# Head 0's preparation in another order over eight banks, with two score tiles begun before the maximum row

## What the reference computes

```python
q = (rmsnorm(c_q, q_latent_g[l]) @ w_uq[l]).reshape(B, T, MLA_HEADS, QK_DIM)
kv = (rmsnorm(c_kv, kv_latent_g[l]) @ w_ukv[l]).reshape(B, T, MLA_HEADS, QK_NOPE + V_DIM)
...
q = rmsnorm(q, q_norm_g[l]); k = rmsnorm(k, k_norm_g[l])      # then rope on the last 32 columns
s = jnp.einsum('bqhd,bkhd->bhqk', qblk, k).astype(jnp.float32) * scale
p = jax.nn.softmax(s, axis=-1).astype(v.dtype)
return jnp.einsum('bhqk,bkhd->bqhd', p, v)
```

## Time and profile before

| | us |
|---|---|
| median of three runs | 1301.13 |
| lowest, highest | 1300.33, 1301.87 |
| the profiled execution | 1303.02 |
| its span | 1301.2 |
| PE busy in it | 1271.2 |

### The profile page before, as it was taken

One profiled execution on the slowest core, in us unless ns is written; L12 is line 12 of the kernel. 1 busy time (PEld: TensorE's weight loads), 2 busy tenths in 40 slices (PEclk: granted clock), 3 DMA queues, 4 the chain that ended last, 5 costly groups with the idle time before them and its releaser, 6 DMA issues.

```text
span 1301.2 us, 18506 instructions
## 1 busy us (share of the span) xinstructions
PE 1271.2 (98%) x6158; PEld 1018.6 (78%) x6158; DVE 996.9 (77%) x1505; ACT 769.3 (59%) x1156; POOL 146.6 (11%) x175
## 2 busy tenths in 40 slices
PE   7999999899999999999999999999999999999998
PEld 7999997666666666687678888888888888888886
DVE  6677569678887876577779887887878887887855
ACT  7487648567765866534445565656474565656460
POOL 3000037400000001322200000000010000000010
PEclk9999999999999999999999999999999999999999
DMA  6111200000000014200144846576574847576667
GB/s 220 34 53 41 74 1 1 1 1 10 9 9 10 9 58 155 69 30 1 49 148 94 187 100 166 118 169 134 151 169 93 189 97 169 113 170 133 157 143 245
DMA packets 40938, 123.01 MB, mean 95 GB/s; under 512 B 7378, under 2 KB 8082, under 8 KB 34484
## 3 DMA queue, kind: packets, MB, share of 16 engines
q0 software_dynamic: 7200, 52.43, 21.4%
q1 hardware_dynamic: 33684, 69.86, 15.7%
HBM read 62.34 MB, written 59.80 MB: 94 GB/s over the span
## 4 chain that ended last, share of the span: by engine, by line
PE 85%; DVE 6%; ACT 5%; issue 2%; DMA 1%; POOL 0%; SPq 0%; DVEq 0%; ACTq 0%
PE banks L2911 30%; PE banks L2983 14%; PE banks L100 7%; PE banks L102 7%; PE banks L101 7%; PE banks L1935 2%; PE banks L2040 2%; PE banks L2041 2%; PE banks L2042 2%; PE banks L2060 2%; PE banks L2063 2%; PE banks L2061 2%; ACT e_f L1558 1%; PE banks L1895 1%; ACT e_h L1565 1%
## 5 line engine op out<-in xcount | busy, mean ns | idle before, releaser
L2911 PE MATMUL banks<-x_hi,slot_h 128*128 128x512 f32 x616 | 242.8, 394 | 2.5 <-DVE slot_l L2599 1.3
L2911 PE MATMUL banks<-x_lo,slot_h 128*128 128x512 f32 x616 | 243.4, 395 | 0.0
L2911 PE MATMUL banks<-x_hi,slot_l 128*128 128x512 f32 x616 | 242.9, 394 | 0.0
L2384 ACT ACTIVATE slot_h<-up_raw 128x512 fp32r<-128x512 f32 x127 | 79.8, 629 | 174.4 <-PE banks L2911 172.3
L2911 PEld LDWEIGHTS banks<-x_hi,slot_h 128*128 128x128 f32 x616 | 115.6, 188 | 30.9 <-DVE slot_l L2599 2.1
L2911 PEld LDWEIGHTS banks<-x_lo,slot_h 128*128 128x128 f32 x616 | 115.7, 188 | 27.1
L2911 PEld LDWEIGHTS banks<-x_hi,slot_l 128*128 128x128 f32 x616 | 115.7, 188 | 26.9
L2462 ACT ACTIVATE staged<-banks 128x1024 f32<-128x1024 f32 x100 | 101.4, 1026 | 41.0 <-PE banks L2983 41.0
L2983 PE MATMUL banks<-dn_h,a_h 128*128 128x512 f32 x280 | 110.4, 394 | 0.0
L2983 PE MATMUL banks<-dn_h,a_l 128*128 128x512 f32 x280 | 109.5, 391 | 0.0
L2983 PE MATMUL banks<-dn_l,a_h 128*128 128x512 f32 x280 | 109.5, 391 | 0.0
(11 more groups left out here) (346 smaller groups left out, 2861.5 us busy)
## 6 DMA issues: line engine op xcount, KB each, us to landing
down_sums<-staged POOLq DMA_DIRECT2D x50, 1024.0 KB, 8.0
up_raw<-in_w_up SPq DMA_DIRECT2D x88, 256.0 KB, 3.3
dn_raw<-in_w_down SPq DMA_DIRECT2D x22, 512.0 KB, 6.6
win_raw<-in_w_in SPq DMA_DIRECT2D x11, 512.0 KB, 3.3
x_tm<-in_x_tm SPq DMA_DIRECT2D x8, 512.0 KB, 6.0
wo_raw<-in_w_out SPq DMA_DIRECT2D x16, 256.0 KB, 4.1
h<-in_x_tm SPq DMA_DIRECT2D x8, 512.0 KB, 5.7
down_sums<-h SPq DMA_DIRECT2D x3, 1024.0 KB, 6.6
```

The lines of the kernel that those rows point to most:

```text
L2384: nc.scalar.activation(s_h[slot], x, ACT.Copy).then_inc(sem["up_hi"], 1)
L2911: ins = nc.tensor.matmul(o, s[slot][:, k], xs[w], start=fresh and k == 0 and n == 0, stop=k == 3 and n == 2, skip_group_check=not fresh)
```

## The change

- The list ahead of head 0 is in another order: `tq0`, `tk0`, `a0`, `a1`, then `tq1`, `tk1`, `a2` to `a7`, `tm`, `a8` to `a15`, `am`, `r`. `x0` to `x2` of head 0 leave it; they are done in slots 1 and 2 of head 0, as for the heads behind.
- `side_banks` names the bank of every job: all eight ahead of head 0, 6 and 7 in turn behind. `before` is the last job ahead of it in the same bank.
- The waits on the projection's semaphores are given by job (`HEAD_0`).
- The identity products now stand before the job's own product: 4 at `tk0`, 4 at `a1`, 2 at each of `a2` to `a15`, 2 at `r`.
- `scores_ahead` makes the three products of all four halves of the score tiles of slots 0 and 1, without the 97th row, behind `r`. `scores` adds to each of them a product of the 97th rows alone once the row has come.

```diff
--- before.py
+++ after.py
@@ -1078,8 +1078,8 @@
                7: ("a14", "a15", "am", "r"), 8: ("", "", "", "")}
     LAST_AHEAD = dict(PREPARE)
     LAST_AHEAD.update({4: ("a5", "x0", "a6", "a7"), 5: ("a8", "x1", "a9", "a10"), 6: ("a11", "x2", "a12", "a13")})
-    FIRST = dict(PREPARE)
-    FIRST.update({8: ("x0", "x1", "x2", "")})
+    FIRST = {0: ("tq0", "tk0", "a0", "a1"), 1: ("tq1", "tk1", "a2", "a3"), 2: ("a4", "a5", "a6", "a7"),
+             3: ("tm", "a8", "a9", "a10"), 4: ("a11", "a12", "a13", "a14"), 5: ("a15", "am", "r", "")}
     OWN = {1: ("", "", "x0", "x1"), 2: ("", "x2", "", "")}
     META_QUERIES = {5: ("xt", "", "", ""), 8: ("", "", "", "xo")}
     LRU_SUMS = {1: ("ys", "", "", "")}
@@ -1091,7 +1091,7 @@
         places = [None] * 4
         ahead = FIRST if h < 0 else LAST_AHEAD if h == END - 1 else PREPARE
         for plan, head in [(ahead, h + 1), (META_QUERIES, h), (LRU_SUMS, h), (OWN, h)]:
-            if plan is OWN and not 1 <= h < END:
+            if plan is OWN and not 0 <= h < END:
                 continue
             if 0 <= head < HEADS and not (plan is META_QUERIES and h != END) and not (plan is LRU_SUMS and h != END - 2):
                 for i, kind in enumerate(plan.get(s, NONE)):
@@ -1104,8 +1104,10 @@
     jobs = [j for h, s in steps for j in side_jobs(h, s) if j]
     number = {j: n for n, j in enumerate(jobs)}
     first = len([j for s in range(SLOTS) for j in side_jobs(-1, s) if j])
+    side_banks = [2, 3, 6, 7, 0, 1, 4, 5] + [(6, 7, 4, 5, 2, 3, 0, 1)[n % 8] for n in range(first - 9)] + [4] +\
+                 [6 + n % 2 for n in range(len(jobs) - first)]
     BY_ACT = {"r", "x0", "x1", "x2"}
-    LOWS = [("tq0", 0), ("tq1", 0), ("tk0", 0), ("tk1", 0)]
+    LOWS = [("tq0", 0), ("tk0", 0), ("tq1", 0), ("tk1", 0)]
     full = [place(f"qk_full{n}", WORDS - 8 - 512 * (n + 1), (512,), parts=QK) for n in range(len(LOWS))]
     assert M_Z <= WORDS - 8 - 512 * len(LOWS)
 
@@ -1117,19 +1119,12 @@
 
     def side_of(j):
 
+        return bank(side_banks[number[j]], 1)
+
+    def before(j):
+
         n = number[j]
-        if n >= first - 3 and n < first:
-            return bank(4 + (n - first + 3) % 2, 1)
-        return bank([6, 7, 2, 3, 0, 1][n % 6] if n < first else 6 + (n - first) % 2, 1)
-
-    def before(j):
-
-        n = number[j]
-        if n < first - 3:
-            return jobs[n - 6:n - 5] if n >= 6 else []
-        if n < first:
-            return jobs[n - 2:n - 1] if n == first - 1 else []
-        return jobs[n - 2:n - 1] if n > first + 1 else [("r", 0), ("am", 0)]
+        return [i for i in jobs[:n] if side_banks[number[i]] == side_banks[n]][-1:]
 
     def hi_upto(j):
 
@@ -1896,8 +1891,10 @@
         ins.then_inc(sem["hn_t"], 1)
 
     def tensor(pe):
-        WARM = {"tk0": 10, "am": 8}
-        WARM.update({f"a{n}": 1 for n in range(2 * XT)})
+        WARM = {"tk0": 4, "a1": 4, "r": 2}
+        WARM.update({f"a{n}": 2 for n in range(2, 2 * XT)})
+        HEAD_0 = {"tq0": (8, 4, 4, 0), "tk0": (8, 4, 4, 0), "a0": (8, 8, 4, 8), "a1": (8, 8, 4, 8),
+                  "tq1": (NT, 8, 8, 8), "tk1": (NT, 8, 8, 8)}
 
         def tile_of(i):
             return slice(P * i, P * i + P) if i < XT else slice(SEQ, T)
@@ -1908,12 +1905,13 @@
             side = side_of(j)
             for i in before(j):
                 wait_read(pe, i)
-            if number[j] < 6 or j == ("tm", 0):
-                done = {"tq0": 8, "tq1": 8, "tk0": 8, "tk1": 8}.get(kind, NT)
-                pe.wait_ge(sem["q_scaled"], done)
-                pe.wait_ge(sem["kv_read"], done)
-                pe.wait_ge(sem["rope_done"], done)
-                pe.wait_ge(sem["v_full"], done)
+            if number[j] < 8 or j == ("tm", 0):
+                for name, done in zip(("q_scaled", "kv_read", "rope_done", "v_full"), HEAD_0.get(kind, (NT,) * 4)):
+                    if done:
+                        pe.wait_ge(sem[name], done)
+            if h == 0 and kind in WARM:
+                for _ in range(WARM[kind]):
+                    nc.tensor.matmul(side[:, 0:P], ident, ident, start=True, stop=True)
             if kind[:2] in ("tq", "tk"):
                 c0 = QK * (h + (HEADS if kind[1] == "k" else 0))
                 for t in range(4):
@@ -1963,11 +1961,6 @@
             elif kind == "xo":
                 ins = meta_columns()
             ins.then_inc(sem["side_done"], 1)
-            if h == 0 and kind in WARM:
-                if kind == "a0":
-                    pe.wait_ge(sem["kv_read"], NT)
-                for _ in range(WARM[kind]):
-                    nc.tensor.matmul(bank(3 if kind == "tk0" else 5)[:, 0:P], ident, ident, start=True, stop=True)
 
         def meta_pv(s, i):
 
@@ -2037,11 +2030,28 @@
                 if g >= 2:
                     pe.wait_ge(sem["e_hi"], g - 1)
             out = s_ps(g)[0:rows(g), cs]
+            if g < 2:
+                ins = nc.tensor.matmul(out, k_h[b][QK:QK + 1, ks], q_h[b][QK:QK + 1, cs], start=False, stop=True)
+                if c == 1:
+                    ins.then_inc(sem["s_done"], 1)
+                return
             nc.tensor.matmul(out, k_h[b][:, ks], q_h[b][:, cs], start=True, stop=False)
             nc.tensor.matmul(out, k_h[b][0:QK, ks], q_l[b][:, cs], start=False, stop=False)
             ins = nc.tensor.matmul(out, k_l[b][:, ks], q_h[b][0:QK, cs], start=False, stop=True)
             if c == 1:
                 ins.then_inc(sem["s_done"], 1)
+
+        def scores_ahead():
+
+            pe.wait_ge(sem["b_set"], 2 + len(LOWS))
+            for g in range(2):
+                ks = slice(P * g, P * g + P)
+                for c in range(2):
+                    cs = slice(512 * c, 512 * c + 512)
+                    out = s_ps(g)[:, cs]
+                    nc.tensor.matmul(out, k_h[0][0:QK, ks], q_h[0][0:QK, cs], start=True, stop=False)
+                    nc.tensor.matmul(out, k_h[0][0:QK, ks], q_l[0][:, cs], start=False, stop=False)
+                    nc.tensor.matmul(out, k_l[0][:, ks], q_h[0][0:QK, cs], start=False, stop=False)
 
         def pv(g, c):
             h, s = divmod(g, SLOTS)
@@ -2066,7 +2076,7 @@
 
         for h, s in steps:
             if (h, s) == (0, 0):
-                pe.wait_ge(sem["b_set"], 2)
+                scores_ahead()
             js = side_jobs(h, s)
             g = SLOTS * h + s
             for c in range(2):
```

## The result

The changed kernel takes **1304.09 us**, median of 17 runs (1301.80 to 1306.05); the kernel before, run beside it on the same chip, takes 1300.27 us (17 runs). The ratio is **1.0029, 95% interval 1.0022 to 1.0037**: 3.8 us slower. I had forecast 1302.8 us, 1.7 us slower, and gave the side "slower by over 0.2%" only 0.19.

What follows compares the result with a forecast made beforehand. PE, busy for 98% of the span, was taken as the bound. Row earlier -1.26, slots 1 to 4 +1.53 and clock +1.4 summed to +1.7 us, 1302.8 us on the median, range 1299.2 to 1304.9 us.

Steps and rivals of the forecast that it cites:

- Row earlier: Ahead of head 0: the new order starts `r` at 243.55 instead of 244.81, so the first score comes 1.26 us earlier.
- Slots 0 to 4: Behind the row in head 0: PE stands at `x0`, slot 4 starts at +14.6 instead of +13.05; 1.5 us lost.
- The one-row products: Behind the row: four products of one row, between 0.03 and 0.23 us each; 0.23 taken.
- The clock: Behind the row: the new gap brings a fall to half clock of 3.4 us; 1.4 us lost.
- The sum: Whole kernel: -1.26 (row), +1.53 (slots 1 to 4), +1.4 (clock) make +1.7 us, 1302.8 us on the median.
- B: Slower rival: clock falls twice, before `a0` and in slot 1; +2.7 us, 1303.8, or 1305.0 at the upper bound; chance 0.2.
- C: Faster rival: PE not held at `x0`, or time won back by slot 4; -1.7 us, 1299.5, down to 1297.6; chance 0.18.
- D: Rival: row lands no earlier, scores ahead only fill the wait; +1.5 us, counted in A's range; chance with A 0.62.
- A: Likeliest case: the sum as forecast, with one clock fall or none; 1301.4 to 1303.6 us; chance with D 0.62.

Runs made afterwards that it cites:

- e5: Changed kernel cut to the new order ahead of head 0; `x0` to `x2` ahead of head 0, scores behind the row as before; ratio 1.0005 to before.
- e3: Changed kernel with seven identity products ahead of the wait of head 0's `x0`; it and its repeat took 1305.06 and 1304.65 us.
- f3: e3 run once more, unedited; the two took 1305.06 and 1304.65 us.
- e2: Changed kernel with `x0` to `x2` of head 0 in slots 4 to 6 instead of 1 and 2; 1300.24 us.
- e6: e5 with one score tile made ahead, behind `x0` to `x2`; the two took 1300.41 and 1300.65 us, which is which not said.
- f2: Kernel before, its own order kept, with slot 0's score tile made ahead behind `x0` to `x2`, `x2` in bank 7; ratio 1.0015 to before.
- f1: e4 with twelve identity products behind `r`, where the changed kernel has its twelve score products; ratio 1.0026 to before.
- e4: Changed kernel without scores made ahead or one-row products, `x0` to `x2` still in slots 1 and 2; time not given, row to slot 4 17.92 us.
- e1: Changed kernel with `x0` to `x2` of head 0 back ahead of head 0, between `r` and the scores made ahead; 1302.36 us.

## Where the prediction was right and where it was wrong

The direction, slower, was right, and so was the mechanism of the loss: the stand at `x0` and the fall of the clock behind it. The size was not. By its own steps:

- **Row earlier, -1.26.** This is the term that was wrong. "`r` ... starts at 243.55, 1.26 us earlier than 244.81" was right in every duration of the new order (`r` 18.85 behind the projections, forecast 19.01). What was wrong is what I set against it: the 244.81 holds the fall at 236. I even said that this fall should go and that its gain is in this term, but I counted as a gain of the change what the unchanged kernel has by itself in another execution: 18.71. The term is **+0.1 to +0.4** (18.85 against 18.71 for `r`, 21.84 against 21.62 for the row; e5's 22.01 against 21.62).
- **Slots 0 to 4, +1.53.** PE stands at `x0` with the scores of slot 2 behind it, for 1.72 us where I had 2.0, released by DVE's `q_l`. Measured with the clock whole, **+1.8** (e3 and f3). By e2 it is the `x` products that cost it: with them out of these slots it is -0.4. That is up to slot 4; at head 1 e3 is only 0.7 us behind e2, whose `x` products then are done too.
- **The one-row products** cost a whole 0.23 each (0.73 for two overlapping records of 0.50), the end of my bounds that I took.
- **The clock, +1.4.** It fell where I said, behind the gap. **+1.9** in one execution and **+1.2** in the other, by how long it stayed low.
- **The sum.** +0.2 + 1.8 + 1.9 (or 1.2) = +3.9 (or +3.2); head 1 starts 3.96 (or 3.31) later behind the projections than in the undisturbed kernel before, and the median is 3.8 later. The forecast's +1.7 was 2.2 short: 1.5 in the first term, 0.3 in the slots, 0.5 in the clock (none with the shorter fall). That the sum meets the median holds only against a before with no fall, and none of its three profiled executions is one: that without the fall at 236 has 6.8 us of it at 420. The mean clocks of the timed executions speak for it; no trace shows it.
- **Luck.** The forecast of 1302.8 us was worked out from a median of 1301.13, and the kernel before, timed beside the changed one, takes 1300.27. So 1302.8 misses 1304.09 by 1.3 us where the difference misses by 2.1. And the upper end of the range, 1304.9, was there for B, whose second fall never came.
- **Rivals.** B had the size, but not by its mechanism: no fall came in the idle stretch ahead of `a0` (PEclk 1.00 there and to 248). C's trigger (slot 4 less than 13 us behind the row) holds only in e2, e6 and f2. D was right in what it said of the row, that it "lands no earlier", and in that the products ahead only fill the wait: f1. I put it inside A's range at +1.5, since I gave it no fall. D with A's fall would have been 0 + 1.5 + 1.4 = +2.9, outside the 0.2%. Both parts were on my page, and I did not add them up.

The Trainium skill (TensorE: Matmul & The Clock Gate, What's actually happening) has activity release the throttle. The runs agree: where the same stretch is filled with identity products (e3, f1), the granted clock stays at 1.00, and where it is not (after, e4), it is 0.50, with 1.2 to 2.6 us lost to it. e1's fall at 254, behind waits no longer than those of e2, which had none, they leave open.

## What to carry to other kernels

Before a term is measured against a stretch of a trace, see whether the clock fell there, and compare two executions of the unchanged kernel: a fall is a throw that differs from one execution to the next, and its price belongs to neither version until both have been seen with and without it. A side job moved to a slot is moved past all in-order queues at once: here `x0` had to wait for a bank behind ACT's and DVE's work on the new head, and took PE's next scores with it; in slots 4 to 6, with the same two banks, that wait is gone. Work put into a wait is worth something only if PE is the late engine where that work is then missing; in slots 0 and 1 ACT is, and twelve products that nobody needs did nearly as well (f1).

## What was not expected of the hardware

- The same kernel, unchanged, had falls at 236, 420 and 536 us in two profiled executions and at 420 (for 6.8 us) and 536 in the third. The fall at 236 costs 1.7 to 1.8 us (23.40 and 23.33 against 21.62), that at 420 0.6 to 1.1 us when it lasts 3.4, and 1.9 when it lasts 6.8.
- Behind the same gap of 1.72 us at `x0` a fall lasted 6.8 us in one execution of the kernel after and 3.4 in the other (252 to 256 us at 0.50 and at 0.66).
- A wait of 2.35 us with nothing of PE's in it brought a fall (e4), one of 1.04 to 1.36 in the same place none (before, e5).
- A product with one contracted row costs as much as one with 97: 0.23 us a stream of 512 columns.
- The chain of stores at the end had some 2 us of room for PE in before: the last result moved by 2.87 us, and the profiled span by 0.2.
